# High and low activations side by side in one 512-column matmul, their two sums added by VectorE

## The chip, the cores and the metric

The kernel runs on one core of a Trainium2 chip. The metric is the device time of one execution in microseconds (us), the median over runs. Every profile is of one execution on that core.

## The reference

The program computes two transformer layers on one sequence of 256 tokens, 2048 features wide. Cut to what matters here, with `@` for the products with the large weight matrices:

```
# first layer: 16 heads of 128, forget-gate attention, then a gated feed-forward with a 3-tap convolution
q, k, v, f = split(rms_norm(x, g0) @ w_in)              # 2048 x (3 * 2048 + 16)
x = x + attention(rms_norm(q), rms_norm(k), v, cumsum(log_sigmoid(f + b))) @ w_out
up = rms_norm(x, g1) @ w_up                             # 2048 x 11264
y = conv3(up); x = x + (silu(y_gate) * y_val) @ w_down  # 5632 x 2048
# second layer: 4 heads of gated linear attention beside 8 heads of dilated attention, gated feed-forward
p = rms_norm(x, g2) @ w_in_2
x = x + concat(gla(p), dilated(p)) @ w_out_2
x = x + (silu(rms_norm(x, g3) @ w_gate) * (rms_norm(x, g3) @ w_up_2)) @ w_down_2
```

All of it is float32. The weights that the `@` products read make up nearly all of the memory traffic.

## The kernel before

**Layout.** Activations lie transposed: features on the 128 partitions, the 256 tokens (`S`) along the free dimension. The residual stream is `xres` [128, 16, 256].

**The weight stream.** All weights are laid out on the host as 788 units of [128, 1024] float32 (512 KB), which is 8 blocks of 128x128. The order of the units is the order of the whole program. For each unit, SyncE loads `raw` (four slots in a ring), ScalarE writes `whi`, the copy rounded to float32r (line 644, `split_hi`), and VectorE writes `wlo = raw - whi` (line 927, `split_lo`). Both do so three units ahead of TensorE (`AHEAD = 3`): the split of unit k+3 stands in their programs at unit k. ScalarE may start on a slot when TensorE has used it up (`unit_used`), VectorE when ScalarE is done, the next load of that slot when VectorE is done.

**The products.** Every activation is also held as two float32r tiles, a rounded high part and the rest as low part (`xs_hi`, `xs_lo` for the normed residual, `mix_hi`, `mix_lo` for the attention output, `hid_hi`, `hid_lo` for the hidden layer). For each 128x128 block, `unit` (lines 324 to 337) issues three 256-column matmuls into the same 256 columns of one PSUM bank: high weights by high activations, high weights by low activations, low weights by high activations (lines 334, 335, 336). Low by low is left out. Each of the three loads its 128x128 weights anew.

**Chunks.** 128 output features by 256 tokens make a chunk: the sum over 16 blocks (two units) of 2048 input features, or over 44 blocks (5.5 units) in the down projections. One layer has 49 chunks into the mixer, 16 out of it, 88 up and 16 down, 169 in all, 338 in both. Four PSUM banks (`acc0` to `acc3`) take chunks in turn. VectorE empties each: `take` (line 953) multiplies it by `rstd` into SBUF, `add_residual` (line 929) adds it to `xres`; one place in the linear-attention heads does it with a scale of its own (line 1058). Each adds one to `chunk_out`, for which TensorE waits before it starts on a bank again, and ScalarE before it reads the result.

**Order.** Each engine's program is written out by hand. TensorE goes through the units and does the small attention matmuls (means, scores, transposes, values) between them, one head later than the projections that feed them. VectorE and ScalarE do the work of a head, or of a pair of up chunks, in fixed steps `s` between their splits. The stages in order of time are: heads of the first layer up to 380 us, out projection, up to 820 us the up projection, then down; the second layer repeats this from 1070 us, with linear-attention heads from 1240 to 1407 us and dilated heads behind them.

Of the kernel before, what the change touches and what calls it, by code (L numbers as in the profile page):

```python
# [30 lines left out]
ALU = mybir.AluOpType  # L31
# [65 lines left out]
def build(nc, wstream, xt, vectors, identity, dist_onehot, rel_bias, gate_w2, scan_keep, gla_mask, fox_mask, out):  # L97
    with ExitStack() as ctx:
# [11 lines left out]
        xs_hi = sb("xs_hi", [P, KC, S], F32R)  # L110
        xs_lo = sb("xs_lo", [P, KC, S], F32R)
# [33 lines left out]
        hid_hi = put("hid_hi", [P, FC, S], F32R)  # L145
        hid_lo = put("hid_lo", [P, FC, S], F32R)
        put, at_att = place(arena)
        mix_hi = put("mix_hi", [P, KC, S], F32R)
        mix_lo = put("mix_lo", [P, KC, S], F32R)
# [64 lines left out]
        chunk_out = sem("chunk_out")  # L214
# [108 lines left out]
        def _(pe):  # L323
            def unit(pos, k, blocks, x_hi, x_lo):
# [14 lines left out]
            def half(pos, k, bank_no, part, x_hi, x_lo, late=None):  # L339
# [3 lines left out]
                              for j in range(BLOCKS)], x_hi, x_lo)  # L343

            def whole(pos, k, bank_no, chunk):
                pe.wait_ge(chunk_out, chunk - 2)
                half(pos, k, bank_no, 0, xs_hi, xs_lo)
                half(pos, k + 1, bank_no, 1, xs_hi, xs_lo)
# [41 lines left out]
            def head(run, pos, h, k0, lag):  # L390
# [3 lines left out]
                whole_q = lambda part: half(pos, k0 + part, 1, part, xs_hi, xs_lo)  # L394
# [9 lines left out]
                half(pos, k0 + 4, 3, 0, xs_hi, xs_lo)  # L404
                if lag >= 1:
                    head_turn(n - 1)
                half(pos, k0 + 5, 3, 1, xs_hi, xs_lo)
# [56 lines left out]
            def gla_head(g, pos):  # L464
# [3 lines left out]
                for c in range(6):  # L468
                    pe.wait_ge(chunk_out, chunk + c - 2)
                    for part in range(2):  # L470
                        half(pos, 2 * c + part, 1 + c % 3, part, xs_hi, xs_lo)
                        after.get(2 * c + part, lambda: None)()

            def project(layer, run):
# [5 lines left out]
                def group(pos, i, tail):  # L480
                    for part in range(2):
                        for c in range(4):
# [9 lines left out]
                            half(pos, 4 * part + c, c, part, mix_hi, mix_lo, late)  # L492
# [8 lines left out]
            def up(layer):  # L501
# [3 lines left out]
                def pairs(pos, i, first):  # L505
                    for j in range(2):
                        for part in range(2):
                            for c in range(2):
# [7 lines left out]
                                half(pos, 4 * j + 2 * part + c, 2 * j + c, part, xs_hi, xs_lo, late)  # L516
# [7 lines left out]
            def down(layer):  # L524

                with pe.Fori(0, 2) as i:
# [3 lines left out]
                    for k in range(U_DOWN // 2):  # L530
# [8 lines left out]
                        unit(pos, k, blocks, hid_hi, hid_lo)  # L539

            for part in range(2):
                half(Pos(0), part, 0, part, xs_hi, xs_lo, {8 * part + j: (xs_ready, 8 * part + j + 1) for j in range(BLOCKS)})
# [8 lines left out]
            for j in range(2):  # L552
                chunk = FOX.chunk0 + 3 * j
                for c, (k, bank_no) in enumerate(((0, 1), (2, 2), (4, 3))):
                    if chunk + c - 2 >= 1:
                        pe.wait_ge(chunk_out, chunk + c - 2)
                    half(Pos(L0.unit_heads), HEAD_UNITS * j + k, bank_no, 0, xs_hi, xs_lo)
# [5 lines left out]
                    half(Pos(L0.unit_heads), HEAD_UNITS * j + k + 1, bank_no, 1, xs_hi, xs_lo)  # L563
# [14 lines left out]
            for part in range(2):  # L578
                half(Pos(L1.unit_in), part, 0, part, xs_hi, xs_lo,
# [12 lines left out]
            for c in range(6):  # L592
                pe.wait_ge(chunk_out, L1.chunk_heads + c - 2)
                for part in range(2):
                    k = 2 * c + part
                    half(Pos(L1.unit_heads), k, 1 + c % 3, part, xs_hi, xs_lo)
# [11 lines left out]
            for j in range(2):  # L608
                chunk = DIL.chunk0 + 3 * j
                n = DIL.count0 + j  # L610
                for c in range(3):
                    pe.wait_ge(chunk_out, chunk + c - 2)
                    for part in range(2):
                        k = 2 * c + part
                        half(Pos(DIL.unit0), HEAD_UNITS * j + k, 1 + c, part, xs_hi, xs_lo)
# [20 lines left out]
        def _(act):  # L636
# [9 lines left out]
            def residual(n, c, chunk):  # L646

                act.wait_ge(chunk_out, chunk + 1)
                act.activation(xs_hi[:, c, :], xres[:, c, :], ACT.Copy, scale=column(f"norm{n}", c)).then_inc(xs_hi_ready, 1)
# [37 lines left out]
            def head_hi(n, at):  # L687
                act.wait_ge(head_copied, n + 1)
                act.activation(mix_hi[:, at, :], head_o[:, :], ACT.Copy).then_inc(mix_hi_ready, 1)
# [28 lines left out]
            def gla_step(g, s, chunk, lag, own=True):  # L718
# [11 lines left out]
                if s == 3 and lag:  # L730
                    act.wait_ge(g_gated, g)
                    act.activation(mix_hi[:, bass.ds(2 * g - 2, 2), :], g_of[:, :, :], ACT.Copy).then_inc(g_hi, 1)
# [24 lines left out]
            def hidden_hi(layer, j):  # L757
                act.wait_ge(hid_ready, FC * layer.n + j + 1)
                act.activation(hid_hi[:, j, :], hid[:, :], ACT.Copy).then_inc(hid_hi_ready, 1)
# [667 lines left out]
```

## Time and profile before

| | |
|---|---|
| median of 3 runs | 2400.36 us (2398.31 to 2400.63) |
| span of the profiled execution | 2396.3 us |
| what lies around the span, by the median | 4.1 us |
| TensorE matmul busy | 2366.9 us (99%), 19522 matmuls |
| TensorE weight loads busy | 2335.3 us (97%), 19522 |
| VectorE busy | 1395.2 us (58%), 2001 instructions |
| ScalarE busy | 1192.7 us (50%), 1574 instructions |
| DMA, mean rate | 177 GB/s, 423.95 MB |

The span runs from the first to the last instruction of the program. The execution that was profiled has no time of its own in the list of runs beside its span. Busy time of TensorE counts matmuls that overlap each other, and so doesn't say how fast it is; starts, or counts over a stretch, do.

### The profile page before, as it was taken

How to read it: one execution, taken by the hardware profiler on the slowest of the kernel's cores; microseconds unless marked ns; L12 is line 12 of the kernel's file. 1: busy time of each engine (PE TensorE's matmuls, PEld its weight loads, DVE VectorE, ACT ScalarE, POOL GpSimd, SP SyncE). 2: the span in 40 equal slices, each digit the busy share in tenths (PEclk: the TensorE clock that was granted, in tenths of full speed). 3: DMA queues.
4: the chain of work that ended last, by engine and by line, in shares of the span. 5: the costliest groups of instructions: out<-in, count | busy, mean ns of one | idle time of the engine just before them, and what ended most of it. 6: DMA issues, size and time to landing. Idle time of an engine off the chain costs nothing.

```text
span 2396.3 us, 50715 instructions
## 1 busy us (share of the span) xinstructions
PE 2366.9 (99%) x19522; PEld 2335.3 (97%) x19522; DVE 1395.2 (58%) x2001; ACT 1192.7 (50%) x1574; POOL 10.4 (0%) x22
## 2 busy tenths in 40 slices
PE   7899999999999999999999999999999999999999
PEld 7899999999999999999999999999999999999999
DVE  6555556676776767554565556565555555554443
ACT  6566665555555555443455466655444444443333
POOL 0000000000000000000000000000000000000000
PEclk9999999999999999999999999999999999999999
DMA  6544445555555555555554444455555555555564
GB/s 235 164 154 157 158 158 182 180 183 183 184 180 182 181 183 184 185 185 177 185 188 148 159 154 159 153 186 183 184 183 179 181 183 184 183 181 197 180 196 135
DMA packets 118083, 423.95 MB, mean 177 GB/s; under 512 B 13597, under 2 KB 15789, under 8 KB 117872
## 3 DMA queue, kind: packets, MB, share of 16 engines
q1 hardware_dynamic: 114048, 415.29, 51.8%
q0 software_dynamic: 1504, 5.12, 0.9%
q10 hardware_dynamic: 2448, 2.32, 0.3%
q8 instruction: 67, 1.10, 0.2%
q14 instruction: 16, 0.13, 0.0%
HBM read 418.98 MB, written 3.69 MB: 176 GB/s over the span
## 4 chain that ended last, share of the span: by engine, by line
PE 96%; DMA 1%; DVE 1%; ACT 1%; issue 1%; SPq 0%; DVEq 0%; ACTq 0%
PE acc L334 31%; PE acc L336 31%; PE acc L335 31%; DMA raw<-wstream 1%; PE b_mean L361 1%; PE b_score L372 0%; DVE wlo L927 0%; ACT whi L644 0%; DMA xres<-xt 0%; PE b_turn L380 0%; PE b_mean L453 0%; PE b_mean L454 0%; PE b_score L371 0%; PE b_mean L386 0%; PE b_mean L388 0%
## 5 line engine op out<-in xcount | busy, mean ns | idle before, releaser
L644 ACT ACTIVATE whi<-raw 128x1024 fp32r<-128x1024 f32 x788 | 830.6, 1058 | 1091.8 <-PE acc L336 1068.2
L927 DVE TENSOR_TENSOR wlo<-raw,whi 128x1024 fp32r<-128x1024 f32 x788 | 962.6, 1224 | 658.2 <-ACT whi L644 656.3
L334 PE MATMUL acc<-xs_hi,whi 128*128 128x256 f32 x4384 | 1258.5, 287 | 13.3 <-DVE wlo L927 11.6
L335 PE MATMUL acc<-xs_lo,whi 128*128 128x256 f32 x4384 | 1242.0, 283 | 0.0
L336 PE MATMUL acc<-xs_hi,wlo 128*128 128x256 f32 x4384 | 1241.8, 283 | 0.0
L334 PEld LDWEIGHTS acc<-xs_hi,whi 128*128 128x128 f32 x4384 | 842.8, 192 | 25.2 <-DVE wlo L927 12.7
L335 PEld LDWEIGHTS acc<-xs_lo,whi 128*128 128x128 f32 x4384 | 843.0, 192 | 5.5 <-issue 5.3
L336 PEld LDWEIGHTS acc<-xs_hi,wlo 128*128 128x128 f32 x4384 | 842.7, 192 | 0.0
L334 PE MATMUL acc<-hid_hi,whi 128*128 128x256 f32 x1408 | 395.2, 281 | 5.1 <-DVE wlo L927 5.1
L336 PE MATMUL acc<-hid_hi,wlo 128*128 128x256 f32 x1408 | 394.7, 280 | 0.0
L335 PE MATMUL acc<-hid_lo,whi 128*128 128x256 f32 x1408 | 394.5, 280 | 0.0
L334 PEld LDWEIGHTS acc<-hid_hi,whi 128*128 128x128 f32 x1408 | 265.7, 189 | 5.5 <-DVE wlo L927 5.5
L336 PEld LDWEIGHTS acc<-hid_hi,wlo 128*128 128x128 f32 x1408 | 265.7, 189 | 0.0
L335 PEld LDWEIGHTS acc<-hid_lo,whi 128*128 128x128 f32 x1408 | 265.5, 189 | 0.0
L334 PE MATMUL acc<-mix_hi,whi 128*128 128x256 f32 x512 | 144.3, 282 | 0.0
L336 PE MATMUL acc<-mix_hi,wlo 128*128 128x256 f32 x512 | 143.3, 280 | 0.0
L335 PE MATMUL acc<-mix_lo,whi 128*128 128x256 f32 x512 | 142.9, 279 | 0.0
L335 PEld LDWEIGHTS acc<-mix_lo,whi 128*128 128x128 f32 x512 | 96.2, 188 | 0.5 <-issue 0.5
L334 PEld LDWEIGHTS acc<-mix_hi,whi 128*128 128x128 f32 x512 | 95.8, 187 | 0.6 <-issue 0.5
L336 PEld LDWEIGHTS acc<-mix_hi,wlo 128*128 128x128 f32 x512 | 96.1, 188 | 0.0
L957 DVE TENSOR_TENSOR up_g<-acc,rstd 128x256 f32<-128x256 f32 x88 | 37.5, 427 | 53.0 <-PE acc L336 48.4
L957 DVE TENSOR_TENSOR up_v<-acc,rstd 128x256 f32<-128x256 f32 x88 | 37.4, 425 | 48.4 <-PE acc L336 48.4
(173 smaller groups left out, 1057.3 us busy)
## 6 DMA issues: line engine op xcount, KB each, us to landing
raw<-wstream SPq DMA_DIRECT2D x788, 512.0 KB, 3.3
xres<-xt SPq DMA_DIRECT2D x4, 512.0 KB, 8.2
decay_row<-decay_scratch POOLq DMA_DIRECT2D x1, 2048.0 KB, 10.7
out<-xres ACTq DMA_DIRECT2D x16, 128.0 KB, 3.4
dist_scratch<-dist_bias POOLq DMA_DIRECT2D x1, 1536.0 KB, 38.3
toeplitz<-dist_scratch POOLq DMA_DIRECT2D x8, 128.0 KB, 4.1
vec<-vectors ACTq DMA_DIRECT2D x1, 213.5 KB, 5.3
g_keep<-scan_keep POOLq DMA_DIRECT2D x1, 128.0 KB, 3.2
```

The lines of the kernel that those rows point to most:

```text
L334: pe.matmul(o, w_hi, x_hi[:, kc, :], start=first, stop=False)
L335: pe.matmul(o, w_hi, x_lo[:, kc, :], start=False, stop=False)
L336: mm = pe.matmul(o, w_lo, x_hi[:, kc, :], start=False, stop=last)
L361: pe.matmul(b_mean[:, :], mean_h[:, :], sq_qk[:, :, :].rearrange("p a s -> p (a s)"), start=True, stop=True).then_inc(qk_mean, 1)
L644: act.activation(whi[slot][:, :], raw[slot][:, :], ACT.Copy).then_inc(hi_ready, 1)
L927: dve.tensor_tensor(wlo[slot][:, :], raw[slot][:, :], whi[slot][:, :], ALU.subtract).then_inc(lo_ready, 1)
L957: dve.tensor_tensor(dst, acc[bank_no][0:rows, 0:S], rstd[0:rows, :], ALU.mult).then_inc(chunk_out, 1)
```

## The change

The two tiles of each activation become one, with the high part and the low part of a feature block next to each other: `xs` [128, 16, 2, 256], `mix` alike, `hid2` [128, 44, 2, 256]. A block is now two matmuls: one of 512 columns, the high weights by both parts, which fills a whole PSUM bank (high product in columns 0 to 255, low product in 256 to 511), and one of 256 columns, the low weights by the high part, added to the second half. The chunk is thus the sum of the two halves of its bank. A new step `fold` on VectorE makes it: a `tensor_reduce` over the two halves, 512 elements in and 256 out, into a new SBUF tile `folded_t`. What emptied the bank before (`take`, `add_residual`, the step in the linear-attention head) reads `folded_t`. Before the fold VectorE waits for its own last chunk (`chunk_out`), behind it for the fold itself (`chunk_folded`).

```
-        xs_hi = sb("xs_hi", [P, KC, S], F32R)
-        xs_lo = sb("xs_lo", [P, KC, S], F32R)
+        xs = sb("xs", [P, KC, 2, S], F32R)
+        folded_t = sb("folded_t", [P, S])
...
-                    o = acc[bank_no][:, 0:S]
-                    pe.matmul(o, w_hi, x_hi[:, kc, :], start=first, stop=False)
-                    pe.matmul(o, w_hi, x_lo[:, kc, :], start=False, stop=False)
-                    mm = pe.matmul(o, w_lo, x_hi[:, kc, :], start=False, stop=last)
+                    pe.matmul(acc[bank_no][:, :], w_hi, x[:, kc, :, :].rearrange("p a s -> p (a s)"), start=first, stop=False)
+                    mm = pe.matmul(acc[bank_no][:, S:2 * S], w_lo, x[:, kc, 0, :], start=False, stop=last)
                 mm.then_inc(unit_used, 1)
...
+            def fold(rows, bank_no, chunk):
+
+                if not isinstance(chunk, int) or chunk:
+                    dve.wait_ge(chunk_out, chunk)
+                dve.tensor_reduce(folded_t[0:rows, :], acc[bank_no][0:rows, :].rearrange("p (a s) -> p s a", a=2),
+                                  AX_X, ALU.add).then_inc(chunk_folded, 1)
+                dve.wait_ge(chunk_folded, chunk + 1)
...
                 dve.wait_ge(unit_used, pos.unit(k))
-                dve.tensor_tensor(xres[:, c, :], acc[bank_no][:, 0:S], xres[:, c, :], ALU.add).then_inc(chunk_out, 1)
+                fold(P, bank_no, chunk)
+                dve.tensor_tensor(xres[:, c, :], folded_t[:, :], xres[:, c, :], ALU.add).then_inc(chunk_out, 1)
...
-                dve.tensor_tensor(dst, acc[bank_no][0:rows, 0:S], rstd[0:rows, :], ALU.mult).then_inc(chunk_out, 1)
+                fold(rows, bank_no, chunk)
+                dve.tensor_tensor(dst, folded_t[0:rows, :], rstd[0:rows, :], ALU.mult).then_inc(chunk_out, 1)
...
-                    dve.scalar_tensor_tensor(out=g_q[:, :], in0=acc[1][:, 0:S], scalar=float(P) ** -0.5, in1=rstd[:, :],
+                    fold(P, 1, L1.chunk_heads + 6 * g)
+                    dve.scalar_tensor_tensor(out=g_q[:, :], in0=folded_t[:, :], scalar=float(P) ** -0.5, in1=rstd[:, :],
```

The rest of the diff gives every caller the new tiles and the number of its chunk. The small attention matmuls, the weight stream and its splits stay as they are.

## Rows read from the trace of the kernel before

**Rows 1.** The page: busy times, and granted clock in 40 slices
```profile
PE 2366.9 (99%) x19522; PEld 2335.3 (97%) x19522; DVE 1395.2 (58%) x2001; ACT 1192.7 (50%) x1574; POOL 10.4 (0%) x22
...
PEclk9999999999999999999999999999999999999999
```

**Rows 2.** The page: chain that ended last, and costliest groups of instructions
```profile
PE 96%; DMA 1%; DVE 1%; ACT 1%; issue 1%; SPq 0%; DVEq 0%; ACTq 0%
...
L644 ACT ACTIVATE whi<-raw 128x1024 fp32r<-128x1024 f32 x788 | 830.6, 1058 | 1091.8 <-PE acc L336 1068.2
L927 DVE TENSOR_TENSOR wlo<-raw,whi 128x1024 fp32r<-128x1024 f32 x788 | 962.6, 1224 | 658.2 <-ACT whi L644 656.3
L334 PE MATMUL acc<-xs_hi,whi 128*128 128x256 f32 x4384 | 1258.5, 287 | 13.3 <-DVE wlo L927 11.6
...
L334 PE MATMUL acc<-hid_hi,whi 128*128 128x256 f32 x1408 | 395.2, 281 | 5.1 <-DVE wlo L927 5.1
...
L334 PE MATMUL acc<-mix_hi,whi 128*128 128x256 f32 x512 | 144.3, 282 | 0.0
```

**Rows 3.** Busy time and counts by stretch: start, out, up, down (first layer)
```profile
core 0: us, PE busy (x) PEld busy (x) DVE busy (x) ACT busy (x) POOL busy (x), PEclk, DMA share, GB/s
0.00:73.00 73.00, 54.54 (x397) 51.42 (x398) 42.32 (x85) 42.52 (x71) 4.60 (x11) 0.98 0.68 216
380.00:430.00 50.00, 50.00 (x427) 50.00 (x426) 31.91 (x47) 25.34 (x36) 0.00 (x0) 1.00 0.54 185
500.00:700.00 200.00, 200.00 (x1669) 200.00 (x1668) 139.87 (x208) 103.09 (x138) 0.00 (x0) 1.00 0.54 182
...
920.00:1060.00 140.00, 140.00 (x1185) 140.00 (x1184) 80.10 (x99) 62.78 (x77) 0.00 (x0) 1.00 0.55 186
```

**Rows 4.** Timeline: weight loads and matmul around a 512-column float32 matmul (start, duration)
```profile
132.84 0.19 PEld L335 LDWEIGHTS acc<-xs_lo,whi 128*128 128x128 f32 x1 [0.24 <-issue]
132.96 0.19 PEld L336 LDWEIGHTS acc<-xs_hi,wlo 128*128 128x128 f32 x1
...
131.99 1.02 PE L361 MATMUL b_mean<-sq_qk,mean_h 128*128 128x512 f32 x2
```

**Rows 5.** Timeline of TensorE in a head's small float32 matmuls
```profile
138.82 0.39 PE L387 MATMUL b_mean<-probs_t,v_tok 128*128 128x128 f32 x2
139.04 0.39 PE L388 MATMUL b_mean<-probs_t,v_tok 128*128 128x128 f32 x2
...
139.81 0.60 PE L372 MATMUL b_score<-qk_n 128*128 128x256 f32 x2
140.25 0.22 PE L374 MATMUL b_score<-maskneg_bf,ident_bf 128*128 128x128 bf16 x1
```

**Rows 6.** Grouped lines by shape: reductions on VectorE
```profile
L977 DVE TENSOR_REDUCE stat<-biased 128x1 f32<-128x256 f32 x24 | 9.8, 409 | 0.0
...
L977 DVE TENSOR_REDUCE stat<-biased 128x1 f32<-128x128 f32 x24 | 6.6, 276 | 0.0
```

**Rows 7.** Timeline of VectorE over one up pair, first layer
```profile
740.98 0.43 DVE L1117 TENSOR_TENSOR hid<-silu_g,tap_v 128x256 f32<-128x256 f32 x1
...
744.10 1.23 DVE L927 TENSOR_TENSOR wlo<-raw,whi 128x1024 fp32r<-128x1024 f32 x1 [1.22 <-ACT whi L644]
745.88 0.43 DVE L957 TENSOR_TENSOR up_g<-acc,rstd 128x256 f32<-128x256 f32 x1 [0.56 <-PE acc L336]
746.98 1.23 DVE L927 TENSOR_TENSOR wlo<-raw,whi 128x1024 fp32r<-128x1024 f32 x1 [0.66 <-ACT whi L644]
748.76 0.42 DVE L957 TENSOR_TENSOR up_v<-acc,rstd 128x256 f32<-128x256 f32 x1 [0.56 <-PE acc L336]
...
749.74 0.48 DVE L1101 SCALAR_TENSOR_TENSOR tap_g<-up_g,vec,tap_g 128x256 f32<-128x256 f32 x1 [0.15 <-DVE tap_g L1098]
...
752.42 0.43 DVE L1117 TENSOR_TENSOR hid<-silu_g,tap_v 128x256 f32<-128x256 f32 x1
```

More of the change, by code:

```diff
@@ L323, in _, with unit @@
         def _(pe):
-            def unit(pos, k, blocks, x_hi, x_lo):
+            def unit(pos, k, blocks, x):
                 slot = pos.slot(k)
@@ L393, in head @@
                 chunk = run.chunk0 + 3 * h
-                whole_q = lambda part: half(pos, k0 + part, 1, part, xs_hi, xs_lo)
+                whole_q = lambda part: half(pos, k0 + part, 1, part, xs)
                 pe.wait_ge(chunk_out, chunk - 2)
@@ L538, in down @@
                             blocks.append((c % 4, kc, kc == 0, kc == FC - 1, late))
-                        unit(pos, k, blocks, hid_hi, hid_lo)
+                        unit(pos, k, blocks, hid2)
             for part in range(2):
-                half(Pos(0), part, 0, part, xs_hi, xs_lo, {8 * part + j: (xs_ready, 8 * part + j + 1) for j in range(BLOCKS)})
+                half(Pos(0), part, 0, part, xs, {8 * part + j: (xs_ready, 8 * part + j + 1) for j in range(BLOCKS)})
             def distance_biases():
@@ L595, in _ @@
                     k = 2 * c + part
-                    half(Pos(L1.unit_heads), k, 1 + c % 3, part, xs_hi, xs_lo)
+                    half(Pos(L1.unit_heads), k, 1 + c % 3, part, xs)
                     if k == 2:
@@ L614, in _ @@
                         k = 2 * c + part
-                        half(Pos(DIL.unit0), HEAD_UNITS * j + k, 1 + c, part, xs_hi, xs_lo)
+                        half(Pos(DIL.unit0), HEAD_UNITS * j + k, 1 + c, part, xs)
                         if not j and k == 0:
@@ L999, in head_step @@
                 if s == 0 and lag >= 1:
-                    take(v_t[:, :], 3, pos.unit(k0 - 1))
+                    take(v_t[:, :], 3, pos.unit(k0 - 1), run.chunk0 + 3 * h - 1)
                     norm_qk(run, n - 1)
@@ L1006, in head_step @@
                         dve.wait_ge(qk_ready, 2 * n)
-                    take(qk[:, 0, :], 1, pos.unit(k0 + 1))
+                    take(qk[:, 0, :], 1, pos.unit(k0 + 1), run.chunk0 + 3 * h)
                     if lag >= 1:
@@ L1014, in head_step @@
                 if s == 4:
-                    take(qk[:, 1, :], 2, pos.unit(k0 + 3))
+                    take(qk[:, 1, :], 2, pos.unit(k0 + 3), run.chunk0 + 3 * h + 1)
             def tail_step(run, s, unit0):
@@ L1020, in tail_step @@
                 if s == 0:
-                    take(v_t[:, :], 3, unit0 - 1)
+                    take(v_t[:, :], 3, unit0 - 1, run.chunk0 + 3 * run.n - 1)
                     norm_qk(run, n - 1)
@@ L1036, in gla_step @@
                 if s == 0 and lag:
-                    take(g_r[:, 1, :], 3, pos.unit(-1))
+                    take(g_r[:, 1, :], 3, pos.unit(-1), L1.chunk_heads + 6 * g - 1)
                 if s == 1 and lag:
@@ L1077, in gla_step @@
                     dve.wait_ge(g_intra, g + 1)
-                    take(g_v[:, 1, :], 1, chunk(3))
+                    take(g_v[:, 1, :], 1, chunk(3), L1.chunk_heads + 6 * g + 3)
                     for t in range(2):
@@ L1082, in gla_step @@
                 if s == 10:
-                    take(g_r[:, 0, :], 2, chunk(4))
+                    take(g_r[:, 0, :], 2, chunk(4), L1.chunk_heads + 6 * g + 4)
                 if s == 11:
@@ L1104, in take_val @@
             def take_val(layer, j, last_unit, bank_no):
-                take(up_v[:, 2:S + 2], bank_no, last_unit)
+                take(up_v[:, 2:S + 2], bank_no, last_unit, layer.chunk_up + 2 * j + 1)
                 if layer.n == 0:
@@ L1202, in project @@
                         if s == 0 or s >= 5:
-                            add_residual(pos, s, 4 * i + c, 0, c % 4)
+                            add_residual(pos, s, 4 * i + c, layer.chunk_out + 4 * i + c, c % 4)
                         split_lo(pos, s)
@@ L1228, in turn @@
                             if s == 3:
-                                take(up_g[:, 2:S + 2], 2 * j, pos.unit(k - 1))
+                                take(up_g[:, 2:S + 2], 2 * j, pos.unit(k - 1), layer.chunk_up + 2 * pair)
                             split_lo(pos, k)
```

76 lines of the change are left out of this document (37 added, 39 removed).

## The prediction, made before the changed kernel was run

> **What bounds the kernel now.** I read the page first: busy times, clock, chain. TensorE and its weight loads are busy 99% and 97%, the granted clock is 1.0 from end to end (the 2.4 GHz level) [rows 1], and 96% of the chain that ended last is TensorE; ScalarE and VectorE mostly wait for TensorE or for each other [rows 2]. So the time is a number of matmuls times the distance of their starts. Busy time can't give that distance: one matmul is listed with 281 to 287 ns, and the next starts long before. The stretches give it [rows 3]: in the up stage 1669 matmuls in 200 us, 120 ns each; in the down and out stages 1185 in 140 us and 427 in 50 us, 118 and 117 ns. Weight loads are as many. The stream has 3 x (4384 + 1408 + 512) = 18912 such matmuls [rows 2], 6304 blocks of three. A block is 360 ns in heads and up stages (4384 blocks) and about 354 ns in down and out (1408 + 512).
>
> **What sets 120 ns.** 256 columns at one per 2.4 GHz clock are 107 ns. The question is where the other 13 go, since the change keeps the columns (768 per block) and drops one matmul and one weight load of three. Around the float32 mean [rows 4], its second half still runs as the next block starts; the load for L335 begins at 132.84, which is when L334 begins to stream, and the next at 132.96, when L335 does. So a load of the next weights starts with a matmul, and the next matmul starts 0.12 us behind it. In the small float32 matmuls, which take two clocks per column [rows 5], the same 107 ns of streaming (128 columns) beside the same load of 128x128 goes at 0.11 us (L387 to L388: two in 0.22), and 256 columns, 213 ns of streaming with one load beside them, at 0.22 us (L372: two in 0.44). The 512-column one takes 0.85 us for two instructions (131.99 to 132.84), 427 ns each, just its streaming [rows 4]. Where streaming is much longer than a load, next to nothing comes on top; where both are near 107 ns, 3 to 13 ns do. I read the 120 ns as the time of a float32r weight load with its hand-over, which sets the distance when the matmul in front is no longer than it.
>
> **TensorE after the change.** High matmul: 512 columns, 213 ns, plus the 3 ns that L372 shows over its streaming (0.22 against 0.213, rounded), 216 ns; the load of the low weights lies inside. Low matmul: 256 columns, during which the next high weights load, 118 ns (117 to 120). Together 334 ns. Saved: 26 ns per block of heads and up, 20 ns in down and out. In the first 73 us (397 matmuls, at most 133 blocks [rows 3]) the start-up bounds, not TensorE; I take these out of the head blocks. (4384 - 133) x 26 = 110.5 us, 1920 x 20 = 38.4 us, together 149 us. The small attention matmuls stay.
>
> The bounds of the two prices: the low matmul can't go below 109 ns (107 and the 3); the high one not below 213. Upwards, if the 13 ns belong to each matmul whatever its length, the block is 2 x 13 + 320 = 346 ns; if they belong to the column (0.469 ns each), it is 360 ns as now, since there are as many columns. The float32 rows speak against both ends, but they feed the array at half the columns per clock, so they don't exclude the column price for float32r. That one stretch runs at 120 and another at 117.5 ns with the same 256 columns [rows 3] speaks against it too: a price of the column would be the same in both.
>
> The Trainium skill, "TensorE: Matmul & The Clock Gate", section "Back-to-back issue gap", gives N / 2.4 + 2.5 ns per warm matmul (109 ns for 256 columns, 216 for 512), and its section "LDWEIGHTS" P / 1.2, 107 ns for 128 columns; a sum by these would be 325 ns per block. The trace has 117 to 120 ns where they give 109, so I don't take them for the low matmul; they are the rival "fully hidden" below.
>
> **VectorE.** Added: 338 folds. Price from the reductions: 409 ns for 256 elements, 276 for 128 [rows 6], 133 ns per 128, so 675 ns for 512. The `take` behind it waits for the fold; VectorE's wait for its own result costs 0.15 us in the rows (L1101 [rows 7]). 0.82 us per chunk, of which 0.675 is busy: 228 us more, VectorE from 1395 to about 1623 us of 2250, 72%. The rows for reductions read SBUF without stride; from PSUM, 256 elements apart, the least is the same 675 ns, the most I allow is two cycles for each element, 2 x 4 x 133 + 143 = 1.2 us. Of two ops of the same size, the one with a PSUM source (L957) takes no longer than the one without (L1117), 0.43 us each [rows 7], so I take 675.
>
> What hides it: VectorE works three units ahead of TensorE, and in the first layer's up stage, its tightest (139.9 us busy of 200 [rows 3]), it still sits idle. One pair of up chunks, 11.5 us, is in [rows 7], hid to hid: 1.22, 0.56, 0.66 and 0.56 us idle for ScalarE's split or TensorE's last matmul, 3.0 us. After: a pair is four units, 32 blocks, 10.69 us (0.83 less), with 1.64 us of folds more. 0.5 us of slack are left, all in waits that must stay (the take can't begin before the chunk ends). It fits. If the fold took 1.2 us, the pair would need 11.2 us, 0.5 more than TensorE, over 44 pairs 23 us. Behind the fold `chunk_out` comes 0.82 us later; TensorE asks for it two or three chunks later (at least 5.3 us), ScalarE's square, tap or residual copy starts that much later, inside a unit of 2.67 us. In the heads the fold of v falls into the 3 us for which VectorE waits for `rstd_qk` anyway.
>
> ScalarE's program is the same (1193 us, 53%). Its split and VectorE's are 1.06 + 1.22 us, due three units later, 8 us instead of 8.6. DMA: 512 KB per 2.67 instead of 2.88 us; its share goes from 0.54 to 0.58, while 0.68 at 216 GB/s was had in the first 73 us [rows 3]. Small losses: one fold at the very end (0.8), one each at the start and at the joins of stages, where TensorE waits for a norm, some tenths in the linear-attention heads, where it now comes earlier to results of ScalarE, and part of the 0.5 us slack above. I put 6 us.
>
> Sum against the profiled span: 2396.3 - 149 + 6 = 2253 us; with the 4.1 us that lie around it by the median of the runs, **2257 us**, 6% faster.
>
> **The rivals.**
> 1. *A fixed price per matmul* (block 346 ns). For: 120 instead of 107 at every one of 18912. Against: the float32 rows, where it is 3. Saves 14 and 8 ns per block: 60 + 15 = 75 us, 2332 us.
> 2. *Load fully hidden* (block 325 ns): the 120 ns come from two nearly equal times that trip each other, and a matmul with its load long done loosens this. For: 109 to 112 in [rows 5]. Against: a weight load still stands next to every low matmul. Saves 35 and 29 ns: 149 + 56 = 205 us. A pair of up chunks would be 10.4 us for TensorE and 10.2 for VectorE, so it is about even there: 2202 us.
> 3. *VectorE becomes the bound in the first up stage*, by the fold at 1.2 us: 23 us there and about 5 in the heads, 2285 us. The skill's "VectorE: DVE Perf Modes", rules for kernel authors, warns of `tensor_reduce` on a hot path as the slowest operation of this engine. By the rows above it costs no more per element than the others, and the rival needs the stride in PSUM to cost.
 It decides from 240 ns for the 512-column matmul on: then block 360, nothing saved in heads and up, 1920 x 6 = 12 us lost in down and out, and the 6 us of folds: 2418 us, slower. Only the rows at 117 to 118 ns stand against it.
>
> **How the numbers follow.** Forecast 0.50, rival 1 0.17, rival 2 0.12, rival 3 0.10, rival 4 0.08, anything else (a wait not seen) 0.03. The likeliest gives 2257 us, by itself 2240 to 2275 (low matmul 115 to 120 ns, losses 2 to 12 us). The range from 2200 to 2338 us takes in rivals 1 to 3 and leaves out the fourth, about 0.12. Faster by over 0.2% (4.8 us, about what runs of this kernel can tell from no change) in all but rival 4 and a part of the rest: 0.89; same 0.02; slower 0.09.
>
> **What would show it.** In the up stage, starts of the high and low matmul 216 and 118 ns apart, and about 1197 matmuls in 200 us (two per 334 ns) in place of 1669. Rival 1: 227 and 120; rival 2: 216 and 109; rival 4: 240 and 120. The fold as a group of 338 with a mean near 0.68 us, and no waits of TensorE for `wlo` outside the start. VectorE idle on `whi` down from 658 us to some 350. Wrong would be a TensorE that waits for VectorE in the first up stage, or a granted clock under 1.0.

## The result, and the profile after

The changed kernel took 2339.8 us (median of 3 runs, 2339.76 to 2339.82) against 2400.36 us: ratio 0.9756, 95% interval [0.9743, 0.9769]. It is 2.4% or 60.5 us faster, where 143 us had been forecast. The direction was right, the size less than half, and the time lies 1.8 us above the upper end of the range. The profiled execution spans 2338.0 us, 58.3 less than the one before.

The page of the changed kernel, its busy times and groups:

```profile
PE 2309.1 (99%) x13218; PEld 1996.5 (85%) x13218; DVE 1609.9 (69%) x2339; ACT 1219.7 (52%) x1574; POOL 10.4 (0%) x22
...
PEclk9999999999999999999999999999999999999999
...
q8 instruction: 31, 0.51, 0.1%
...
L331 PE MATMUL acc<-xs,whi 128*128 128x512 f32 x4384 | 1552.7, 399 | 14.9 <-DVE wlo L923 12.4
...
L923 DVE TENSOR_TENSOR wlo<-raw,whi 128x1024 fp32r<-128x1024 f32 x788 | 961.0, 1222 | 417.4 <-ACT whi L640 414.5
L332 PE MATMUL acc<-xs,wlo 128*128 128x256 f32 x4384 | 1221.2, 279 | 0.0
...
L929 DVE TENSOR_REDUCE folded_t<-acc 128x256 f32<-128x512 f32 (+1 forms) x338 | 233.0, 689 | 159.3 <-PE acc L332 143.7
```

6304 matmuls and as many weight loads are gone (x19522 to x13218) [rows 1], TensorE is still busy 99%, and the clock stays at its upper level. The fold costs 689 ns, close to the 675 forecast. VectorE's idle time on `whi` fell from 656 to 414 us [rows 2] (forecast: some 350). TensorE waits for `wlo` 12 us in all, as before: nobody else has become the bound. So what remained of the forecast gain is inside the matmul stream. The stretches of the changed kernel: up stage of the first layer, its down stage, and out:

```profile
core 0: us, PE busy (x) PEld busy (x) DVE busy (x) ACT busy (x) POOL busy (x), PEclk, DMA share, GB/s
442.00:922.00 480.00, 480.00 (x2771) 419.81 (x2770) 405.34 (x606) 275.75 (x353) 0.00 (x0) 1.00 0.57 189
930.00:1170.00 240.00, 240.00 (x1378) 210.19 (x1378) 138.03 (x158) 105.36 (x121) 0.00 (x0) 1.00 0.59 189
372.00:437.00 65.00, 65.00 (x370) 56.62 (x369) 47.41 (x70) 33.67 (x47) 0.00 (x0) 1.00 0.57 188
```

Two matmuls are a block: 346 ns in the up stage (2 x 480 / 2771), 348 in down, 351 in out. A count takes in the matmuls cut by the ends of its window and so reads a little low in short ones; the starts themselves give 346.7, 348.9 and 353.3, and for the kernel before 360.0, 353.4 and 353.4. The forecast was 334 in all of them.

The same starts correct the stage times given for the kernel before: its first out stage runs from 355 to 449 us, the up stage from there to 956, the down stage to 1209, where the second layer begins. So the window from 920 to 1060 us in [rows 3] holds 36 us of the up stage, and the down stage alone has 117.8 ns per matmul, like out. How the changed block splits is in the timeline of TensorE, first in out, then in up:

```profile
399.61 0.40 PE L331 MATMUL acc<-mix,whi 128*128 128x512 f32 x1
399.84 0.28 PE L332 MATMUL acc<-mix,wlo 128*128 128x256 f32 x1
399.96 0.40 PE L331 MATMUL acc<-mix,whi 128*128 128x512 f32 x1
400.20 0.28 PE L332 MATMUL acc<-mix,wlo 128*128 128x256 f32 x1
400.32 0.39 PE L331 MATMUL acc<-mix,whi 128*128 128x512 f32 x1
...
599.92 0.40 PE L331 MATMUL acc<-xs,whi 128*128 128x512 f32 x1
600.15 0.28 PE L332 MATMUL acc<-xs,wlo 128*128 128x256 f32 x1
600.27 0.39 PE L331 MATMUL acc<-xs,whi 128*128 128x512 f32 x1
600.50 0.27 PE L332 MATMUL acc<-xs,wlo 128*128 128x256 f32 x1
600.61 0.40 PE L331 MATMUL acc<-xs,whi 128*128 128x512 f32 x1
```

High to low is 0.23 us and low to the next high 0.12. The low matmul has about the price forecast (118). The high one does not: about 230 ns, not 216. Out repeats at 0.35 and 0.36, up at 0.35 and 0.34: the same two instructions with the same operand shapes in two rhythms.

The span's 58.3 us by stage, from the starts of TensorE's first matmul in each: up 37.5 (two stages), heads 6.5, down 14.2, out 0. The 6.5 are about 11 us gained in the heads, less some 4 lost in the first 70 us and some 1 where the second layer begins. The down figure is more than the block allows: 1408 blocks x 4.5 ns are 6. The rest was found at one place of the kernel before, between the two passes of its down loop:

```profile
1080.07 0.28 PE L335 MATMUL acc<-hid_lo,whi 128*128 128x256 f32 x1
1080.18 0.28 PE L336 MATMUL acc<-hid_hi,wlo 128*128 128x256 f32 x1
1083.02 0.38 PE L334 MATMUL acc<-hid_hi,whi 128*128 128x256 f32 x1 [2.56 <-DVE wlo L927]
...
1083.82 0.41 PE L334 MATMUL acc<-hid_hi,whi 128*128 128x256 f32 x1
1084.03 0.41 PE L335 MATMUL acc<-hid_lo,whi 128*128 128x256 f32 x1
```

Two starts lie 2.84 us apart where 0.12 would do, so 2.7 us are lost, and a little later the matmuls start 0.21 us apart. The profile puts the wait down to `wlo`, but VectorE had finished 353 of its splits by 1080.05, and TensorE went on with the 351st unit: `wlo` isn't what it waited for. The windows of the kernel before on it:

```profile
1079.00:1083.00 4.00, 1.46 (x13) 1.25 (x11) 2.83 (x4) 1.76 (x3) 0.00 (x0) 1.00 0.61 230
1083.00:1088.00 5.00, 4.98 (x29) 4.99 (x30) 0.60 (x2) 0.29 (x1) 0.00 (x0) 0.66 0.34 111
```

The granted clock falls to a mean of 0.66 right after the gap, that is, to the lower level (1.2 GHz) for part of it. 29 matmuls in 5 us where 42 would go: 1.6 us more, 4.3 us per gap in all. There is one in each down stage (the other near 2265 us), and the changed kernel has neither.

### The profile page after: what moved, and what is told of

Its sections match the earlier page's. It is cut to its first block, busy times and chain, and to the rows that moved or that the text cites. A ratio compares the mean times of both kernels' runs of the same rounds, so it can differ in the third digit from the quotient of the medians.

```text
span 2338.0 us, 39013 instructions
## 1 busy us (share of the span) xinstructions
PE 2309.1 (99%) x13218; PEld 1996.5 (85%) x13218; DVE 1609.9 (69%) x2339; ACT 1219.7 (52%) x1574; POOL 10.4 (0%) x22
## 4 chain that ended last, share of the span: by engine, by line
PE 95%; DMA 2%; DVE 2%; ACT 1%; issue 1%; SPq 0%; DVEq 0%; ACTq 0%
PE acc L331 61%; PE acc L332 30%; DMA raw<-wstream 2%; PE b_mean L357 1%; DVE wlo L923 1%; PE b_score L368 0%; DMA xres<-xt 0%; PE b_turn L376 0%; ACT whi L640 0%; PE b_mean L449 0%; PE b_mean L450 0%; PE b_score L367 0%; PE b_mean L382 0%; PE b_mean L383 0%; PE b_mean L384 0%
## 5 line engine op out<-in xcount | busy, mean ns | idle before, releaser
L331 PE MATMUL acc<-xs,whi 128*128 128x512 f32 x4384 | 1552.7, 399 | 14.9 <-DVE wlo L923 12.4
L923 DVE TENSOR_TENSOR wlo<-raw,whi 128x1024 fp32r<-128x1024 f32 x788 | 961.0, 1222 | 417.4 <-ACT whi L640 414.5
L332 PE MATMUL acc<-xs,wlo 128*128 128x256 f32 x4384 | 1221.2, 279 | 0.0
L331 PEld LDWEIGHTS acc<-xs,whi 128*128 128x128 f32 x4384 | 825.4, 188 | 217.6 <-DVE wlo L923 14.4
L332 PEld LDWEIGHTS acc<-xs,wlo 128*128 128x128 f32 x4384 | 827.4, 189 | 5.8 <-issue 5.6
L331 PE MATMUL acc<-hid,whi 128*128 128x512 f32 x1408 | 491.3, 393 | 0.0
L332 PE MATMUL acc<-hid,wlo 128*128 128x256 f32 x1408 | 394.5, 280 | 0.0
L929 DVE TENSOR_REDUCE folded_t<-acc 128x256 f32<-128x512 f32 (+1 forms) x338 | 233.0, 689 | 159.3 <-PE acc L332 143.7
L331 PEld LDWEIGHTS acc<-hid,whi 128*128 128x128 f32 x1408 | 264.9, 188 | 61.0
L332 PEld LDWEIGHTS acc<-hid,wlo 128*128 128x128 f32 x1408 | 263.6, 187 | 0.0
L331 PE MATMUL acc<-mix,whi 128*128 128x512 f32 x512 | 182.6, 398 | 0.0
L963 DVE TENSOR_TENSOR up_v<-folded_t,rstd 128x256 f32<-128x256 f32 x88 | 37.5, 426 | 3.0
```

Source lines behind the costliest of these rows:

```text
L331: pe.matmul(acc[bank_no][:, :], w_hi, x[:, kc, :, :].rearrange("p a s -> p (a s)"), start=first, stop=False)
L332: mm = pe.matmul(acc[bank_no][:, S:2 * S], w_lo, x[:, kc, 0, :], start=False, stop=last)
L923: dve.tensor_tensor(wlo[slot][:, :], raw[slot][:, :], whi[slot][:, :], ALU.subtract).then_inc(lo_ready, 1)
L929: dve.tensor_reduce(folded_t[0:rows, :], acc[bank_no][0:rows, :].rearrange("p (a s) -> p s a", a=2), AX_X, ALU.add).then_inc(chunk_folded, 1)
L963: dve.tensor_tensor(dst, folded_t[0:rows, :], rstd[0:rows, :], ALU.mult).then_inc(chunk_out, 1)
```

## The experiments

The theories after the result. **A**: the price sits on the matmul, 13.3 ns on top of its columns for every float32r matmul, whatever its length (rival 1). **B**: the high matmul would cost 216, but something in the kernel, such as the streams of ScalarE and VectorE, slows it. And two side questions: do the folds cost anything, and what is the gap in the down stage. The expectations quoted below letter their own theories anew; A and B in the text between them are these two. Ratios are to runs of the kernel before that were made beside each experiment (medians 2397.81, 2398.12 and 2399.09 us), not to the 2400.36 above.

**One: the forms of matmul by themselves** (`e1_forms`). A kernel that computes nothing of the reference: one block of weights and activations is loaded, and TensorE runs rows of 96 (192 for the float32 instructions) matmuls, one form after the other, the other engines still until the last row.

```
for i in range(96): pe.matmul(o(i), wt(w_r, i), x_r[:, 0:512], ...)                     # L81, and 256 columns L85
for i in range(96): pe.matmul(o(i), wt(w_b, i), x_b[:, 0:512], ...)                     # L93 bfloat16, 256 columns L95
for i in range(96):
    pe.matmul(o(i), wt(w_r, i), x_r[:, 0:512], ...)                                     # L101, the changed kernel's block
    pe.matmul(o(i, 256, 512), wt(w_r, i + 4), x_r[:, 0:256], ...)                       # L102
```

> A kernel of matmuls alone: 96 of each form back to back on TensorE, each with a weight load of its own, ScalarE and VectorE idle (its output is not the reference's; no part of the network is computed). Forms: float32r with 512, 384, 256 and 128 columns; 512 and 256 columns with 64 instead of 128 weight columns; bfloat16 512 and 256; float32 512 and 256; then the block of the changed kernel (512 and 256 float32r), the same with the low matmul in bfloat16, the block of the kernel before (three of 256), and last the changed block again while ScalarE and VectorE stream 1024-element instructions. Theory A, the price belongs to the column of a float32r stream (0.451 ns): 231 ns for 512 columns, 173 for 384, 115 for 256; the same with 64 weight columns; bfloat16 512 at 216. Theory B, the price belongs to each float32r matmul with its weight load (13.3 ns): 227, 173, 120; pair 347, three 360; fewer with 64 weight columns. Theory C, the price comes from the weight load only where the stream in front is no longer than it (the prediction's reading): 216, 163, 118. Theory D, it comes from the other engines' use of SBUF: 216 and 109 while they are idle, 231 and 115 in the last form.

Its time was 455.2 us. The distance of starts of one form is the time from first to last start over the 95 steps between them (191 for float32). The rows by line of this kernel give count, duration (minimum, median, maximum) and first and last start:

```profile
L81 PE MATMUL acc<-x_r,w_r x96: 389/389/582, 34.6 to 56.3; 128*128 128x512 f32 x96
L85 PE MATMUL acc<-x_r,w_r x96: 278/283/283, 73.2 to 84.6; 128*128 128x256 f32 x96
L87 PE MATMUL acc<-x_r,w_r x96: 224/274/280, 84.7 to 95.3; 128*128 128x128 f32 x96
L93 PE MATMUL acc<-x_b,w_b x96: 379/379/390, 128.4 to 148.9; 128*128 128x512 bf16 x96
L95 PE MATMUL acc<-x_b,w_b x96: 272/273/273, 149.1 to 159.5; 128*128 128x256 bf16 x96
L97 PE MATMUL acc<-x_raw,w_raw x192: 592/592/595, 159.6 to 241.6; 128*128 128x512 f32 x192
```

float32r: 229 ns for 512 columns (the usual step is 227), 174 for 384 and 120 for 256, that is 13 to 16 ns over 213, 160 and 107. For 128 columns it is 111, which is 58 over 53. bfloat16: 216 and 109, 213 + 3 and 107 + 2. float32: 429 ns for each instruction, 427 + 2. From 256 columns up, the 13 ns neither grow with the columns nor vanish behind a longer stream. At 128 columns the distance no longer follows the columns, and 111 ns may be a floor of the kind that the prediction had in mind; the 120 ns of 256 columns lie above it. So "whatever its length" in A holds for the two lengths of this kernel and not below. The sentence of the forecast "where streaming is much longer than a load, next to nothing comes on top" holds for float32 and bfloat16, and not for float32r. Blocks, by windows of this kernel: the pair of the change, three matmuls of 256, and the pair again while the other two engines work without a pause:

```profile
284.00:314.00 30.00, 30.00 (x175) 26.44 (x174) 0.00 (x0) 0.00 (x0) 0.00 (x0) 1.00 0.00 1
...
352.00:382.00 30.00, 30.00 (x253) 30.00 (x252) 0.00 (x0) 0.00 (x0) 0.00 (x0) 1.00 0.00 1
387.00:417.00 30.00, 30.00 (x171) 26.04 (x170) 30.00 (x28) 30.00 (x32) 0.00 (x0) 1.00 0.00 1
```

By their starts: 346.7, 360.0 and 353.4 ns. The bare pair has the up stage's block, and three have the old one. The slower pair beside busy engines left B alive for the 7 ns.

**Two: is it the other engines?** (`e4_phases`). The same pair, 96 times each: all still, VectorE alone, ScalarE alone, both, and then behind different short rows of other matmuls.

```
for i in range(2): pe.matmul(o(i, 0, 256), wt(w_raw, i), x_raw[:, 0:256], ...)          # float32, ahead of the row at L110
for i in range(96):
    pe.matmul(o(i), wt(w_r, i), x_r[:, 0:512], ...)
    pe.matmul(o(i, 256, 512), wt(w_r, i + 4), x_r[:, 0:256], ...)
```

> Matmuls alone again (the output is not the reference's). The block of the changed kernel (512 + 256 columns) took 347 ns in the up stages and 353 in the out stages, and in the isolated forms 347 with ScalarE and VectorE idle, 353 with both streaming. Here the same block 96 times: idle, VectorE alone streaming, ScalarE alone, both, then idle again behind three float32 matmuls of 128 columns, behind two of 256, behind one in bfloat16; then in another order (two of 512, two of 256); then the old block of three, also behind one in bfloat16. Theory contention: 347 in all idle stages and 353 or more in those with an engine streaming. Theory phase (how the weight loads and matmuls fall against each other when a stretch begins, kept until the next break): 347 and 353 in stages of either kind, changed by what stands in front, and 360 or 353 for the old block.

```profile
24.00:54.00 30.00, 30.00 (x172) 26.02 (x171) 0.00 (x0) 0.00 (x0) 0.00 (x0) 1.00 0.00 1
58.00:88.00 30.00, 30.00 (x172) 26.02 (x171) 28.39 (x26) 0.00 (x0) 0.00 (x0) 1.00 0.00 1
92.00:122.00 30.00, 30.00 (x172) 26.00 (x171) 0.00 (x0) 27.24 (x29) 0.00 (x0) 1.00 0.00 1
...
160.00:190.00 30.00, 30.00 (x172) 26.00 (x171) 0.00 (x0) 0.00 (x0) 0.00 (x0) 1.00 0.00 1
195.00:225.00 30.00, 30.00 (x175) 26.21 (x174) 0.00 (x0) 0.00 (x0) 0.00 (x0) 1.00 0.00 1
```

353.4 ns with everything still, with VectorE, with ScalarE, and with both; still 353.4 behind three float32 matmuls of 128 columns (the row from 160 us) and behind one in bfloat16; 346.7 in the last row shown, behind two float32 matmuls of 256 columns. So B is refuted: the pair has two rhythms here and keeps the one in which it begins, whatever the other engines do (in the kernel the up stage has 346.7 with both at work). It began in the faster one each time float32 matmuls of 256 columns stood in front: here, in `e1_forms`, and behind one, two, three and four of them in `e5_widths`. Why a beginning leads into the one or the other was not found. Two high ones and two low ones in turn took 348 ns a block. The old block of three took 360.0 ns in both of its rows here, as in `e1_forms`. Its 353.4 of the out and down stages stand in no isolated row; a difference that was not tested is the tile from which the activations are read.

**Three: the high matmul cut in two** (`e2_three`). The changed kernel with its layout and folds, and the old three matmuls:

```diff
-                    pe.matmul(acc[bank_no][:, :], w_hi, x[:, kc, :, :].rearrange("p a s -> p (a s)"), start=first, stop=False)
+                    pe.matmul(acc[bank_no][:, 0:S], w_hi, x[:, kc, 0, :], start=first, stop=False)
+                    pe.matmul(acc[bank_no][:, S:2 * S], w_hi, x[:, kc, 1, :], start=False, stop=False)
```

> The changed kernel with its layout and its folds, but the high matmul cut into two of 256 columns, so that a block is three matmuls again, 18912 in all. By the isolated forms (13.3 ns for each float32r matmul with its weight load, over N / 2.4 GHz) a block is 360 ns again. Theory B (the whole gain is the third load): the time of the kernel before, 2400 us, within 5, folds hidden; the 120 ns interval back in the up stage. Rival, the folds cost 10 us or more of the path: 2410 us and more. Second question, the pauses of 4 us in each down stage of the kernel before that the changed one lacks: if they come with the length of TensorE's loop body (1056 matmuls against 704), they are back here; if they come with something of the old layout, they are not, and the time is 8 us lower, 2392.

2401.49 us (2396.12 to 2403.08), ratio to the kernel before 1.0013 [1.0003, 1.0022]. The up stage has the old count back, as in [rows 3], and so are both gaps of the down stages:

```profile
500.00:700.00 200.00, 200.00 (x1669) 200.00 (x1668) 163.63 (x245) 109.12 (x141) 0.00 (x0) 1.00 0.55 182
```

The whole gain of the change is in the number of matmuls, each with its weight load; the run doesn't part the two. Folds and layout cost 3 us by this ratio. By the starts of the units the profiled execution falls behind the one before by 2.9 us in its first 90 us and by 1.2 us at the beginning of the linear-attention heads.

**Four: no folds** (`e3_no_folds`). The changed kernel with each chunk read from the first half of its bank alone. It leaves out the second half of the banks, the two products with a low part.

```diff
-                fold(P, bank_no, chunk)
-                dve.tensor_tensor(xres[:, c, :], folded_t[:, :], xres[:, c, :], ALU.add).then_inc(chunk_out, 1)
+                dve.tensor_tensor(xres[:, c, :], acc[bank_no][:, 0:S], xres[:, c, :], ALU.add).then_inc(chunk_out, 1)
```

> The changed kernel without the 338 folds: each chunk is taken from the first half of its bank alone, so the second half (both products with a low part) is left out of the result. If the folds are hidden beside TensorE, as predicted: 2339 us, at most 2 us under the changed kernel (one fold at the end, one or two at the joins). If VectorE holds TensorE up somewhere, 10 us or more under it.

2338.5 us (2334.9 to 2339.17), ratio 0.975 [0.9732, 0.9767], the same as with the folds within the intervals. VectorE's idle time on `whi` grows by what the folds took:

```profile
DVE wlo L923 <- ACT whi L640: 623.3, 591, 5.5
```

against 414.5 us. Nearly all of the 233 us of new work on VectorE were hidden. By the starts of the units it gains 2.9 us on the changed kernel at the start and 1.2 at the beginning of the linear-attention heads, just what `e2_three` lost there; it has the new layout too, so these 4 us are the price of the folds. It loses 3 us in the second down stage, which fell into the slower rhythm: 1332 matmuls in 235 us in place of 1349. That shows how a small edit elsewhere can move the rhythm, and it hides the 4 us in the total.

**Five: weights narrower, matmuls grouped** (`e5_widths`). Again rows of matmuls by themselves: weights 32, 64, 96 and 128 columns wide, and eight high matmuls followed by eight low ones, float32r or bfloat16.

> Matmuls alone (the output is not the reference's). First the work of a unit grouped: 8 high matmuls of 512 columns, then 8 low ones of 256, the low ones in bfloat16 (twice, the second behind a break), all in float32r (twice), and in bfloat16 with the activations read as the upper halves of the float32r words; then 256 and 512 columns of float32r with 32, 64, 96 and 128 weight columns; then the block of the changed kernel behind one, two, three and four float32 matmuls of 256 columns. If the price lies in the weight load's columns (one clock of the stream for each 4 of them): 3.3, 6.7, 10 and 13.3 ns over N / 2.4 GHz. If it is one of the instruction: 13.3 ns for all widths. Grouped: 336 ns a block in bfloat16 plus the price of two changes of type per unit (from the mixed pair of the isolated forms, 356 - 336 = 20 ns for two, so 2.5 per block: 338), 347 to 353 in float32r. Behind the breaks: 347 or 353, by the phase.

The rows by line of this kernel, 48 matmuls each, 256 and 512 columns with weights 32 wide, 256 columns with 64, then both with 128:

```profile
L104 PE MATMUL acc<-x_r,w_r x48: 279/280/366, 189.3 to 194.9; 128*32 128x256 f32 x48
L106 PE MATMUL acc<-x_r,w_r x48: 391/394/397, 195.0 to 205.9; 128*32 128x512 f32 x48
L108 PE MATMUL acc<-x_r,w_r x48: 276/276/280, 206.2 to 211.5; 128*64 128x256 f32 x48
...
L116 PE MATMUL acc<-x_r,w_r x48: 278/283/283, 239.3 to 244.9; 128*128 128x256 f32 x48
L118 PE MATMUL acc<-x_r,w_r x48: 389/389/398, 245.0 to 255.7; 128*128 128x512 f32 x48
```

Over 47 steps, at widths 32, 64, 96 and 128: 120, 114, 116 and 120 ns for 256 columns, 232, 230, 230 and 227 for 512. A quarter of the weight columns doesn't make it cheaper, and at 512 columns the full width is the cheapest, so the width of the load is not the price. But half the width takes 6 ns off the 256-column matmul (in `e1_forms` too, 114 ns), so the 13 ns aren't the same at every width. Grouped in eights a block is 343 ns with low matmuls in bfloat16, 346 where these read the upper halves of float32r words, and 351 all in float32r. Alternating them one by one is dearer: in `e1_forms` a bfloat16 low matmul behind each float32r one moved the high one to about 320 ns and left 39 for the low, 358 in all, more than with one type. The price of changing type is paid once per group.

**Six and seven: grouping in the kernel** (`e6_group_r`, `e7_group_b`). A unit issues its eight high matmuls and then its eight low ones; in the second the low ones are bfloat16, with `wlo` written in that type and the high activations read as the upper halves of their words. This is the second; the first keeps its `mm` line as it was:

```diff
+                    pe.matmul(acc[bank_no][:, :], w_hi, x[:, kc, :, :].rearrange("p a s -> p (a s)"), start=first, stop=False)
+                for j, (bank_no, kc, first, last, late) in enumerate(blocks):
                     w_lo = wlo[slot][:, j * P:(j + 1) * P]
-                    pe.matmul(acc[bank_no][:, :], w_hi, x[:, kc, :, :].rearrange("p a s -> p (a s)"), start=first, stop=False)
-                    mm = pe.matmul(acc[bank_no][:, S:2 * S], w_lo, x[:, kc, 0, :], start=False, stop=last)
+                    top = x[:, kc, 0, :].bitcast(BF16).rearrange("p (s t) -> p s t", t=2)[:, :, 1]
+                    mm = pe.matmul(acc[bank_no][:, S:2 * S], w_lo, top, start=False, stop=last)
```

> The changed kernel with the matmuls of a unit grouped, 8 high ones, then 8 low ones, all still float32r; the same columns and the same weight loads. If the price is 13.3 ns for each matmul with its load, wherever it stands: 347 to 353 ns a block as now, 2340 us, within 6 (only the phase can differ). If the order of long and short matmuls counts (a load behind a short matmul costs, behind a long one is hidden, as the prediction had it): another time by 10 us or more.

> The same grouping, with the low matmuls in bfloat16: VectorE writes the low weights as bfloat16, and the activations are read as the upper two bytes of the float32r words already there, so no engine does anything more. The low product is rounded to bfloat16 factors. The isolated forms have 109 ns for such a matmul against 120. Theory B: 338 instead of 347 to 353 ns a block: 2816 x 8 in the up stages, 512 x 15, 1408 x 11, some 1500 x 12 in the heads, 64 us less: 2276 us, between 2265 and 2300. Rival: reading every second bfloat16 costs the stream, or the changes of type cost more than 20 ns per unit: 2340 us or more.

2333.59 us (2333.56 to 2334.44), ratio 0.9734 [0.9713, 0.9754], and 2327.04 us (2325.93 to 2327.27), ratio 0.9704 [0.9684, 0.9725]: 6 and 13 us better than the changed kernel (for the first the two intervals overlap). The second is far from the 2276 us that bfloat16's own price had promised. Up and down stage of the second:

```profile
440.00:918.00 478.00, 478.00 (x2759) 364.51 (x2758) 403.68 (x604) 274.31 (x350) 0.00 (x0) 1.00 0.57 189
930.00:1160.00 230.00, 230.00 (x1329) 176.03 (x1327) 130.86 (x148) 100.76 (x114) 0.00 (x0) 1.00 0.59 190
```

A block is 346.5 and 346.1 ns by these counts, the up stage's no shorter than the changed kernel's. All in float32r, `e6_group_r` has 349.1 ns in up, 344.7 in down and 346.5 in out by its starts: the order moves the price a little each way, which a fixed one doesn't foresee. The timeline of that kernel, whose groups of one line stand in one row, shows one unit:

```profile
1760.44 1.09 PE L334 MATMUL acc<-xs,wlo 128*128 128x256 bf16 x8
1761.27 2.09 PE L330 MATMUL acc<-xs,whi 128*128 128x512 f32 x8
1763.21 0.52 PE L334 MATMUL acc<-xs,wlo 128*128 128x256 bf16 x3
```

Eight low matmuls take 0.83 us, eight high ones 1.94, 2.77 us in all where 8 x (109 + 227) = 2.69 had been counted on. The single starts of this unit part the 85 ns between them: a high matmul follows a high one after 224 to 236 ns in place of 227 (33 ns in all), a low one a low one after 114 in place of 109 (28 ns), and the two changes of type cost 24 ns. The 114 ns go with the strided reading: `e5_widths` has 114 for such low matmuls too, and 109 where the bfloat16 elements stand side by side. What the version gains on the changed kernel lies in the heads (3 us per layer), out (1.7) and down (1.6) and not in up: these are the stages in which that kernel's block is over 346.7 ns. It is the fastest of this study.

**Eight and nine: the gap in the down stage.** In `e8_no_down_loop` the kernel before has its two passes written out instead of looped. In `e9_down_cut` the changed kernel's high matmul is cut in two in the down stages alone.

```diff
-                with pe.Fori(0, 2) as i:
-                    pos = Pos(layer.unit_down, U_DOWN // 2, i)
+                for i in range(2):
+                    pos = Pos(layer.unit_down + i * U_DOWN // 2)
```

> The kernel before with TensorE's two passes over a down stage written out one behind the other in place of a loop; the order and number of the matmuls are the same. In the profile before TensorE stands still once in each down stage, for 2.8 us near 1080 us and for 2.8 us near 2265 us, between the two passes, and the changed kernel has neither gap. Theory A, the jump back: a pass of 1056 matmuls and as many weight loads is more than the engine keeps at hand, and going back to its start makes it wait for the instructions to be read again. Then both gaps go and the time falls by 6 to 9 us, to 2389 to 2394 us, with more instruction packets than the 67 of before. Theory B, the rate of reading: 256-column matmuls use up instructions faster than they are brought. Then written-out code has the same gaps or more, and the time stays within 2 us of 2400 or is longer.

> The changed kernel with the 512-column high matmul cut into two of 256 columns in the two down stages alone, 1408 blocks. Its pass through a down stage then has 1056 matmuls again in place of 704. Theory A, a fixed price per matmul and a pause at a pass of over about a thousand matmuls: the gap of about 3 us comes back once in each down stage (8 us in all with the slower units behind it), and a unit of a down stage goes back from 2.79 to 2.83 us, 7 us over 176 units: about 2355 us, 15 us over the changed kernel, all of it in the down stages. Rival: the pauses belong to something else that the change removed, such as the hidden products by VectorE: no gap, 2347 us.

2390.41 us (2389.59 to 2391.75), ratio 0.9966 [0.9954, 0.9978], and 2353.94 us (2351.5 to 2355.04), ratio 0.9813 [0.9799, 0.9826]. The same two stretches as above in the first of them, then the place of the first gap in the second:

```profile
1079.00:1083.00 4.00, 4.00 (x36) 4.00 (x35) 1.65 (x2) 2.08 (x3) 0.00 (x0) 1.00 0.56 155
1083.00:1088.00 5.00, 5.00 (x45) 5.00 (x44) 3.18 (x4) 2.17 (x5) 0.00 (x0) 1.00 0.55 194
...
1058.00:1062.00 4.00, 1.34 (x10) 1.14 (x10) 3.46 (x6) 1.87 (x3) 0.00 (x0) 0.95 0.53 179
```

Written out, the same matmuls run through at full clock, and 8.7 us of the kernel before are gone. In the changed kernel the gap returns with the third matmul in both down stages, 14 us in all with the longer blocks. So it is the jump back over a pass of 1056 matmuls and 1056 weight loads; over 704 and 704 there is none. The pages count 67 instruction packets for the kernel before, 31 for the changed one and 58 for `e9_down_cut`, which fits a pass that is read again; `e8_no_down_loop` has 62, where more than 67 had been expected, so the packets alone don't settle it. The Trainium skill, "Runtime: NRT & Kernel Launch", section "Instruction fetch mechanics", says that TensorE holds 2048 instructions and that a taken branch whose target is not in the current window makes the engine wait for a fetch. The runs agree on both sides of that size (2112 and 1408, waits not counted). The price measured here is 2.7 us between two starts and 1.6 us more at the lower clock; that what TensorE waited for was the reading of instructions is argued from these runs, no row shows it.

## Why the prediction was wrong

**The step that failed** is the price of the high matmul: "213 ns, plus the 3 ns that L372 shows over its streaming", 216 ns. It measured 227 alone, 230 in the block, so the block is 346.7 ns where 334 was summed. The 3 ns came from float32 rows, and the forecast itself had the warning in hand: 11 to 13 ns at each of 18912 float32r matmuls. (The rows it read have two decimals and give 0.22 - 0.213 = 7 ns; the 3 are right for float32, as `e1_forms` showed with 216, but [rows 5] couldn't say so.) It explained them by a weight load as long as the stream ahead of it, a reading which the kernel before, with only one length of float32r matmul, could neither support nor refute. The runs put about 13.3 ns on the float32r matmul at 256, 384 and 512 columns with weights 128 wide. What inside the engine takes them, and whether they belong to the matmul or to the weight load that each one has, stays open.

**The sum again, term by term.** Up: 2816 blocks, forecast 26 ns each, 73 us; measured 13, 37 us. Heads: forecast 37 us; measured some 11, since many of their blocks run at 353. Down: forecast 28 us; 6 from the block (4.5 ns each) and 8.6 from the two gaps that nobody had foreseen, less 0.8 for the fold at the very end. Out: forecast 10 us; nothing, for the old block was 353.4 ns and the new one runs in the slow rhythm at 353.3. Losses: forecast 6 us; about 4 at the start and 1 at the second layer's beginning, most of it the folds. At the start the clock stood at 0.93 in place of 0.98 [rows 3]:

```profile
0.00:73.00 73.00, 51.98 (x250) 42.01 (x251) 45.07 (x90) 40.44 (x68) 4.60 (x11) 0.93 0.67 212
```

The saving in out and down was counted from 354 ns, 6 below up, and taken to end at the same 334. The measured blocks differ by stage too, and why the old block has 353.4 ns there wasn't found.

**The rivals.** The fixed price (rival 1, chance 0.17) was the right mechanism for the two lengths of this kernel and gave 2332 us, 8 us too good: it took 346 ns for every block, and the slower rhythms in heads and out cost more than the gaps gave back. *Load fully hidden* is refuted by `e1_forms`. Its rule in the Trainium skill ("TensorE: Matmul & The Clock Gate", section "Back-to-back issue gap"), N / 2.4 + 2.5, which the section gives as the gap of single matmuls, is met by the bfloat16 rows, 216 and 109 ns, and misses the float32r rows of 256 to 512 columns by about 11 and that of 128 by 55. VectorE as the bound is refuted by the fold at 689 ns and by `e3_no_folds`. A price of the column is refuted by 227 ns for 512 columns, where it needed 240.

**What was right**: TensorE's stream as the only bound and the count of blocks, the low matmul at 118 (117 to 119), the fold's price and that it lies under other work (VectorE 69% busy, 72% forecast), no new wait of TensorE for `wlo`.

## What to carry to other kernels

Before a sum rests on one price times thousands of instructions, take that price from rows of the same type: float32r pays about 13 ns for each matmul of 256 to 512 columns, so fewer and wider matmuls save some 13 ns each and no more. A loop on TensorE whose pass has over a thousand matmuls with their loads should be cut smaller or written out, here 4.3 us for each jump back (704 cost nothing; between the two nothing was measured). Extra work on an engine with a third of its time idle can be nearly free: of 233 us some 4 came through, at the places where TensorE waits for that engine's results.

## What the runs showed that was not expected

- A price by type, at 256 and 512 columns: float32r 13.3 ns over its columns, bfloat16 and float32 2 to 3. At 128 columns float32r took 111 ns, 58 over its columns.
- Two rhythms of the same alternating pair, 346.7 and 353.4 ns, each kept for all 96 blocks, with all other engines still; the kernel's down stage has a third, 348.9.
- A jump back over 2112 instructions stops TensorE for 2.7 us, and the clock then falls to its lower level for part of the next 5 us.
- Alternating float32r and bfloat16 matmuls one by one costs 358 ns a block, eight by eight 343.
